# A recurrence's decay exponentials moved ahead of the next tile's gates, with TensorE's order changed to match, and one copy moved in the seventh unit

## The chip, the cores and the metric

The kernel runs on one core of a Trainium2 chip. The metric is the device time of one execution in microseconds (us), as the median of several. The core has five engines that run their own instruction lists in order and meet at semaphores: TensorE (PE in the profile; its weight loads are PEld), VectorE (DVE), ScalarE (ACT), GpSimd (POOL) and SyncE (SP), which here only issues DMAs.

## The reference, cut to what matters

One inference step of a one-layer backbone over 512 latent and 128 context tokens of width 1024. What the change touches is the token mixer:

```python
proj = h @ w_in                               # seven groups of 512 columns
xr, gr, q_raw, ff, fb, iv, og = split(proj)
xc = depthwise_conv(xr, conv_w, conv_b, row_len)
# RG-LRU, forward and backward over the tokens
r = sigmoid(blockdiag(xc, w_a) + b_a); i = sigmoid(blockdiag(xc, w_x) + b_x)
log_a = -8 * r * softplus(-lam);  a = exp(log_a)
u = sqrt(-expm1(2 * log_a)) * (i * xc)
h[t] = a[t] * h[t-1] + u[t]
y_lru = rmsnorm(h_f + h_b) * gelu(gr)
# HGRN2, 4 heads x 2 directions: a chunked gated linear attention
```

Behind it come the output projection, a router and a mixture of 16 experts, which is the longer half of the time.

## The kernel before, in words

Tokens are laid out as 640 columns (512 latent, 128 context); feature channels lie on the 128 partitions. Every engine's list is written out by hand, so the order in the text is the order of the run, and a wait holds up all that is behind it on its engine.

The **first recurrence** (RG-LRU) has four channel tiles j = 0 to 3 and two directions d. For one tile TensorE makes `gates(j, d)`: 16 small products into two PSUM areas. Only (0, 1) has areas of its own, all the others share one pair, so `gates(j, d)` waits until ScalarE has taken the gates before it (`gate_in`). ScalarE's `lru_gates(j)` takes four sigmoids out of PSUM and makes two tanh; `lru_exp(j)` makes the decay `a`, two exponentials; `lru_root(j)` two square roots; `lru_square(j)` the square of the tile's sum for the norm. VectorE's `lru_in(j)` multiplies the input gate by xc, squares the decay (L1645) and forms z (L1648), then `lru_scan(j)` runs the scans (L1655 to L1664) and signals `lru_done`, for which `lru_gates(j + 2)` waits, since tiles j and j + 2 share buffers. VectorE's order is `lru_in(0)`, a swap of halves, `lru_in(1)`, a swap, `lru_scan(0)`, `lru_scan(1)`, and the same for tiles 2 and 3 without the swaps.

TensorE fills the time between gates with the **input projections** of the second recurrence: `HEAD0` = Q, OG, FF, FB, V of head 0, and `EARLY`, the FF of head 1. `project_sample` is 16 matmul instructions of 512 columns (8 steps of k, two instructions each; `range(0, 4)` is half of them), `project_prompt` is 16 of 128 columns and signals `full`. Two PSUM areas alternate; `wait_pa` waits for ScalarE's `projected(item)`, which empties them. `lru_sum` sums the squares over the partitions (it waits for VectorE's `lsq_done`) and feeds the norm's logarithm. On ScalarE `projected(EARLY)` stands just ahead of that logarithm, and it waits for EARLY's `full`:

```python
            act.wait_ge(conv_done, LT + 2)
            projected(EARLY)

            act.wait_ge(ln_ps, 1)
            A(a2[0], p45[:, 0:T], ACT.Ln, bias=eps[:, 0:1], scale=1.0 / (LT * P)).then_inc(ln_log, 1)
```

The **second recurrence** (HGRN2) has eight units u (head u // 2, direction u % 2). In each, ScalarE makes ten exponentials (the last groups are the three `LEVELS`, 64, 32, 16, and W[5]); it copies the turned values out of PSUM (`v_tok`, `vt_done`) and the turned keys (`k_tok`, `kt_done`). TensorE turns the values (`turn_v`, L707), does projections, turns the keys (`turn_k`, L714, into the PSUM area that the values were in, so it waits for `vt_done`), and then `updates`, `scores` and `outputs`. In units 0, 1, 3 and 5 an `ada_copy` on ScalarE feeds an `ada_turn` on TensorE (L621), which stands between the keys and `updates`.

Of the kernel before, what the change touches and what calls it, by code (L numbers as in the profile page):

```python
# [14 lines left out]
KT = D // P  # L15
# [71 lines left out]
def program(nc, x_prompt, x_sample, state_lru, state_hgrn, c, c_ctx, w_ada, b_ada, norm_mix, w_in,  # L87
# [7 lines left out]
    with ctx:  # L95
# [465 lines left out]
        def _(pe):  # L561
# [14 lines left out]
            def project_sample(item, ks=range(KT)):  # L576
                g, j = item
                n, s = USE[item], wait_load(("in", g))
                if ks[0] == 0:
                    wait_pa(n)  # L580
                for k in ks:
                    r = mm(pa[n % 2][:, 0:TS], ring[:, s, k, j * P:(j + 1) * P], hT[:, k, 0:TS], k == 0, k == KT - 1)
                if g == IN_GR and ks[-1] == KT - 1:
                    r.then_inc(full, 1)

            def project_prompt(item):
                g, j = item
                if g == IN_GR:
                    return
                n, s = USE[item], SLOT_OF[("in", g)][0]  # L590
                for k in range(KT):
                    r = mm(pa[n % 2][:, TS:T], ring[:, s, k, j * P:(j + 1) * P], hT[:, k, TS:T], k == 0, k == KT - 1)
                r.then_inc(full, 1)
                if j == HEADS - 1:
                    pe.wait_ge(full, n + 1)
                    pe.sem_inc(freed[s], 1)

            def project(item):
                project_sample(item)
                project_prompt(item)  # L600
# [59 lines left out]
            def gates(j, d):  # L660

                n = 4 * j + 2 * d
                pe.wait_ge(conv_done, (2, 4, 7, 8)[j])
                if n == 0:
                    pe.wait_ge(s_wbd, 16 * 9)
                    pe.wait_ge(xr_in, LT)
                elif n == 2:
                    pe.wait_ge(xr_in, LT)
                else:
                    pe.wait_ge(gate_in, n if n > 4 else 2)  # L670
                for a, b in ((0, TS), (TS, T)):
                    for hf in range(2):
                        for g in range(2):
                            at, out = 64 * (hf ^ g), 64 * hf
                            r = mm(gate_at(j, d, g)[out:out + 64, a:b], wbd[at:at + 64, g, d, j, out:out + 64],
                                   (xc[j], x_swap[j % 2])[g][at:at + 64, a:b])
                r.then_inc(gate_ps, 2)

            def lru_sum():

                pe.wait_ge(lsq_done, LT + 1)
                pe.wait_ge(gate_in, 4 * LT)
                mm(p45[:, 0:TS], ones[:, :], sq[0][:, 0:TS])
                mm(p45[:, TS:T], ones[:, :], sq[0][:, TS:T]).then_inc(ln_ps, 1)
                nc.tensor.transpose(p67[0:8, 0:P], lru_last[:, :, :].rearrange("p d j -> p (d j)"), ident[:, :]).then_inc(lst_ps, 1)
# [174 lines left out]
            gates(0, 0)  # L860
            gates(0, 1)
            gates(1, 0)
            project_sample(HEAD0[0], range(0, 4))
            gates(1, 1)
            project_sample(HEAD0[0], range(4, KT))
            project_prompt(HEAD0[0])
            project(HEAD0[1])
            gates(2, 0)
            project_sample(HEAD0[2])
            gates(2, 1)  # L870
            project_prompt(HEAD0[2])
            gates(3, 0)
            project_sample(HEAD0[3], range(0, 4))
            gates(3, 1)
            project_sample(HEAD0[3], range(4, KT))
            project_prompt(HEAD0[3])
            project(HEAD0[4])
            project(EARLY)
            lru_sum()

            for u in range(UNITS):
                fill = FILL[u]
# [302 lines left out]
        def _(act):  # L1185
# [78 lines left out]
            def lru_gates(j):  # L1264
                b = j % 2
                if j >= 2:
                    act.wait_ge(lru_done, j - 1)
                for d in range(2):
                    for g in range(2):
                        n = 4 * j + 2 * d + g  # L1270
                        act.wait_ge(gate_ps, n + 1)
                        A((rg, ig)[g][b][d], gate_at(j, d, g)[:, 0:T], ACT.Sigmoid,
                          bias=col(("lru_ba", "lru_bx")[g], 4 * d + j)).then_inc(gate_in, 1)
                if j == 0:
                    act.wait_ge(sp_done, 1)
                for d in range(2):
                    act.wait_ge(gate_in, 4 * j + 2 * d + 1)
                    A(th[b][d], rg[b][d], ACT.Tanh, scale=sp[:, 3, 4 * d + j:4 * d + j + 1]).then_inc(gates_done, 1)

            def lru_exp(j):  # L1280
                b = j % 2
                act.wait_ge(gates_done, 2 * j + 2)
                for d in range(2):
                    A(rg[b][d], rg[b][d], ACT.Exp, scale=sp[:, 4, 4 * d + j:4 * d + j + 1]).then_inc(a_done, 1)
# [11 lines left out]
            def projected(item):  # L1296
# [8 lines left out]
                else:  # L1305
                    m = {IN_Q: 2, IN_FF: 0, IN_FB: 1, IN_V: 3}[g]
                    A(raw[h % 2][m], src, ACT.Silu if g == IN_Q else ACT.Copy).then_inc(e, 1)

            lru_gates(0)
            lru_gates(1)  # L1310
            lru_exp(0)
            lru_exp(1)
            projected(HEAD0[0])
            lru_root(0)
            lru_root(1)
            projected(HEAD0[1])
            lru_gates(2)
            lru_gates(3)
            lru_exp(2)
            lru_exp(3)  # L1320
            projected(HEAD0[2])
            lru_square(0)
            lru_square(1)
            lru_root(2)
# [25 lines left out]
            for u in range(UNITS):  # L1350
                h, d = u // 2, u % 2
                rw, fill = raw[h % 2], FILL[u]
                normed = h - 1 if d == 0 and h >= 1 else None
                if u == 0:
                    act.wait_ge(lru_y, 1)
                else:
                    act.wait_ge(o_ps, u)
                if d == 0:
                    for g in (IN_Q, IN_FF, IN_FB, IN_V):
                        n = USE[(g, h)]  # L1360
                        act.wait_ge(empty[n % 2], n // 2 + 1)
                f = rw[d]
                for o, i_ in seq(f, d):
                    r = A(W[6][:, o], i_, ACT.Sigmoid)
                chain(r)
                for o, i_ in seq(f, d):
                    r = A(kk[:, o], i_, ACT.Sigmoid, scale=-1.0)
                chain(r)
                A(lf, W[6], ACT.Ln, bias=lb[:, 4 * d + h:4 * d + h + 1], scale=oml[:, 4 * d + h:4 * d + h + 1]).then_inc(lfk, 1)
                if d == 1:  # L1370
                    for o, i_ in seq(rw[2], d):
                        r = A(rw[1][:, o], i_, ACT.Copy)
                    for o, i_ in seq(rw[3], d):
                        r = A(rw[0][:, o], i_, ACT.Copy)
                    r.then_inc(qrev, 1)
                if normed is not None:
                    head_square(normed)
                    head_log(normed)
                if d == 1 and u < UNITS - 1:
                    projected(fill[0])  # L1380

                act.wait_ge(cum_done, u + 1)
                A(decay[:, :], cum[:, P - 1::P], ACT.Exp)
                act.wait_ge(sub_done, 5 * u + 1)
                A(W[6], W[6], ACT.Exp, scale=-1.0).then_inc(exp_done, 1)
                act.wait_ge(sub_done, 5 * u + 2)
                chain(A(W[4], W[3], ACT.Exp, scale=-1.0))
                A(W[3], W[3], ACT.Exp).then_inc(exp_done, 1)
                for lv, hs in enumerate(LEVELS):
                    act.wait_ge(sub_done, 5 * u + 3 + lv)  # L1390
                    v = W[lv].rearrange("p (g x) -> p g x", x=2 * hs)
                    A(v[:, :, 0:hs], v[:, :, 0:hs], ACT.Exp, scale=-1.0)
                    A(v[:, :, hs:2 * hs], v[:, :, hs:2 * hs], ACT.Exp).then_inc(exp_done, 1)
                A(W[5], cum, ACT.Exp).then_inc(exp_done, 1)
                if normed is not None:
                    head_rstd(normed)
                act.wait_ge(vt_ps, u + 1)
                A(v_tok, p67[:, 0:T], ACT.Copy).then_inc(vt_done, 1)
                if d == 0 or u == UNITS - 1:
                    projected(fill[0])  # L1400
                for item in fill[1:-1]:
                    projected(item)
                act.wait_ge(kt_ps, u + 1)
                A(k_tok, p67[:, 0:512], ACT.Copy).then_inc(kt_done, 1)
                if u in ADA_UNIT:
                    ada_copy(ADA_UNIT[u])
                projected(fill[-1])
# [666 lines left out]
```

## Time and profile before

| | |
|---|---|
| time, median of 3 runs | 1004.91 us (1004.6 to 1005.25) |
| the profiled execution's own time | 1005.39 us, of which the span of the trace is 1003.7 us |
| PE busy | 963.6 us (96%) |
| DVE busy | 362.8 us (36%) |
| ACT busy | 291.8 us (29%), 63 table loads |
| mean granted TensorE clock | 0.992 |

Times in the trace are from the span's start. The first recurrence lies between about 67 us and 138 us, unit 0 of the second between 138 us and 166 us, unit 6 (the seventh) between 321 us and 346 us, and the experts from about 480 us to the end.

### The profile page before, as it was taken

How to read it: one execution, taken by the hardware profiler on the slowest of the kernel's cores; microseconds unless marked ns; L12 is line 12 of the kernel's file. 1: busy time of each engine (PE TensorE's matmuls, PEld its weight loads, DVE VectorE, ACT ScalarE, POOL GpSimd, SP SyncE). 2: the span in 40 equal slices, each digit the busy share in tenths (PEclk: the TensorE clock that was granted, in tenths of full speed). 3: DMA queues.
4: the chain of work that ended last, by engine and by line, in shares of the span. 5: the costliest groups of instructions: out<-in, count | busy, mean ns of one | idle time of the engine just before them, and what ended most of it. 6: DMA issues, size and time to landing. Idle time of an engine off the chain costs nothing.

```text
span 1003.7 us, 18297 instructions
## 1 busy us (share of the span) xinstructions
PE 963.6 (96%) x7982; PEld 429.9 (43%) x7982; DVE 362.8 (36%) x825; ACT 291.8 (29%) x485; POOL 101.8 (10%) x112
## 2 busy tenths in 40 slices
PE   5999899999999899997999999999999999999996
PEld 3555556666666554462232332322323223232232
DVE  4477666463653663663021020210212102112115
ACT  5137756573653754323010010100101001010012
POOL 3200010000000011212001102011010110200100
PEclk9999999999999999999899999999999999999999
DMA  9990013504028441136799999999999999999982
GB/s 332 331 384 7 1 38 142 174 6 169 6 90 316 198 150 73 74 126 238 308 428 403 415 419 411 419 395 415 422 393 418 396 411 416 399 418 401 411 346 105
DMA packets 49396, 276.07 MB, mean 275 GB/s; under 512 B 4001, under 2 KB 12353, under 8 KB 37057
## 3 DMA queue, kind: packets, MB, share of 16 engines
q1 hardware_dynamic: 42000, 253.24, 62.7%
q0 software_dynamic: 5824, 16.81, 5.7%
q10 hardware_dynamic: 1520, 5.28, 1.4%
q8 instruction: 39, 0.64, 0.3%
q14 instruction: 13, 0.10, 0.0%
HBM read 262.30 MB, written 13.01 MB: 274 GB/s over the span
## 4 chain that ended last, share of the span: by engine, by line
PE 83%; DVE 7%; ACT 3%; DMA 3%; issue 2%; POOL 1%; SPq 0%; POOLq 0%; DVEq 0%
PE pa L563 53%; PE p L563 26%; DMA ring<-in_w_ada_dram 1%; ACT reg_c L1195 1%; DMA h_rows<-reg_d 1%; PE pa L1085 1%; ACT L1195 1%; PE p L1023 1%; ACT reg_b L1195 1%; DVE reg_c L1613 1%; DVE reg_c L1658 1%; POOL reg_d L505 0%; ACT reg_d L1195 0%; DMA reg_c<-h_rows,row_s 0%; PE pa L1028 0%
## 5 line engine op out<-in xcount | busy, mean ns | idle before, releaser
L563 PE MATMUL pa<-ring,reg_b 128*32 128x512 f32 (+1 forms) x3232 | 412.8, 595 | 1.3 <-ACT reg_b L1195 1.2
L563 PEld LDWEIGHTS pa<-ring,reg_b 128*32 128x32 f32 (+1 forms) x3232 | 128.6, 114 | 256.5 <-issue 256.0
L563 PE MATMUL pa<-reg_a,ring 128*128 128x512 f32 (+1 forms) x768 | 227.1, 449 | 5.9 <-DVE reg_a L1550 3.3
L563 PE MATMUL p<-ring,reg_b 128*16 128x512 f32 x1536 | 172.7, 594 | 0.0
L563 PEld LDWEIGHTS pa<-reg_a,ring 128*128 128x128 f32 x768 | 118.1, 191 | 98.4 <-issue 98.3
L1195 ACT ACTIVATE reg_b<-pa 128x512 f32<-128x512 f32 (+1 forms) x36 | 21.0, 608 | 426.9 <-PE pa L563 262.6
L563 PEld LDWEIGHTS p<-ring,reg_b 128*16 128x16 f32 x1536 | 44.9, 97 | 121.0 <-issue 120.3
L1952 DVE TENSOR_TENSOR reg_b<-reg_b,p 128x512 f32<-128x512 f32 x8 | 5.5, 687 | 234.4 <-PE p L563 234.4
L1195 ACT ACT_TABLE_LOAD x63 | 80.8, 1283 | 4.1 <-issue 2.8
L1976 DVE SCALAR_TENSOR_TENSOR reg_c<-pa,slot_s,reg_c 128x512 f32<-128x512 f32 x14 | 10.5, 751 | 101.5 <-PE pa L563 101.5
L1195 ACT ACTIVATE reg_c<-reg_c 128x320 f32<-128x320 f32 (+1 forms) x86 | 43.3, 574 | 10.1 <-DVE reg_c L1664 9.2
L541 POOL DMA_INDIRECT sum_rows<-reg_c,row_s x7 | 10.3, 1476 | 262.5 <-DVE reg_c L1976 262.5
L1692 DVE SCALAR_TENSOR_TENSOR reg_c<-reg_c,oml 128x320 f32<-128x320 f32 (+1 forms) x40 | 27.1, 681 | 20.5 <-ACT reg_c L1195 20.5
L1696 DVE TENSOR_TENSOR reg_c<-reg_c 128x640 f32<-128x640 f32 x40 | 30.1, 820 | 0.3
L1983 DVE SCALAR_TENSOR_TENSOR reg_c<-p,slot_q,reg_c 16x512 f32<-16x512 f32 x28 | 20.9, 746 | 20.0 <-PE p L563 19.7
L1960 DVE TENSOR_TENSOR reg_b<-reg_b,pa 128x512 f32<-128x512 f32 x16 | 11.0, 688 | 44.1 <-PE pa L563 44.1
L563 PE MATMUL p<-ring,cs 128*2 128x128 f32 x768 | 24.4, 282 | 2.6 <-DMA ring<-in_w_ada_dram 2.4
L1195 ACT ACTIVATE reg_d<-pa 128x640 f32<-128x640 f32 (+2 forms) x24 | 15.1, 639 | 34.6 <-PE pa L563 34.4
L1692 DVE SCALAR_TENSOR_TENSOR reg_c<-reg_d,reg_c 128x320 f32<-128x320 f32 (+1 forms) x40 | 24.1, 619 | 0.0
L563 PEld LDWEIGHTS p<-ring,cs 128*2 128x2 f32 x768 | 19.5, 87 | 10.7 <-issue 6.4
L1718 DVE TENSOR_TENSOR_SCAN reg_c<-ones,reg_c 128x128 f32<-128x128 f32 x40 | 13.5, 404 | 25.1 <-ACT reg_c L1195 25.1
L563 PE MATMUL p<-reg_c 128*16 128x16 f32 (+3 forms) x640 | 21.6, 202 | 0.0
(304 smaller groups left out, 750.4 us busy)
## 6 DMA issues: line engine op xcount, KB each, us to landing
ring<-in_w_gate_dram SPq DMA_DIRECT2D x32, 2048.0 KB, 13.7
ring<-in_w_up_dram SPq DMA_DIRECT2D x32, 2048.0 KB, 14.1
ring<-in_w_down_dram SPq DMA_DIRECT2D x32, 2048.0 KB, 17.6
ring<-in_w_ada_dram SPq DMA_DIRECT2D x8, 2048.0 KB, 8.2
ring<-in_w_in_dram SPq DMA_DIRECT2D x6, 2048.0 KB, 20.9
ring<-in_w_ada_dram SPq DMA_DIRECT2D x8, 1024.0 KB, 11.5
ring<-in_w_out_dram SPq DMA_DIRECT2D x2, 2048.0 KB, 19.1
sum_rows<-reg_a ACTq DMA_DIRECT2D x5, 512.0 KB, 2.7
```

Source lines behind the costliest of these rows:

```text
L541: pool.indirect_dma_start(sum_rows, bass.IndirectOffsetOnAxis(row_s[0:CS, i:i + 1], 0), out_s[0:CS, :], None, compute_op=ALU.add).then_inc ...
L563: return nc.tensor.matmul(out, lhsT, rhs, start=start, stop=stop, **kw)
L1023: r = nc.tensor.transpose(p67[:, k * P:(k + 1) * P], xg_s[:, k * P:(k + 1) * P], ident[:, :])
L1085: r = nc.tensor.transpose(dst[:, f * P:(f + 1) * P], src[:, f * P:(f + 1) * P], ident[:, :])
L1195: return nc.scalar.activation(out, in_, f, **kw)
L1613: V.scalar_tensor_tensor(dst_s, a_s, wt, dst_s, ALU.mult, ALU.add)
L1692: return V.scalar_tensor_tensor(dst, src, s, dst, ALU.mult, ALU.mult)
L1696: V.tensor_tensor(dst.rearrange("p (g x) -> p g x", x=x), c3, c3[:, :, at:at + 1].to_broadcast([P, T // x, x]), ALU.subtract).then_inc(sub ...
L1718: r = V.tensor_tensor_scan(cum[:, n * P:(n + 1) * P], ones[:, :], lf[:, n * P:(n + 1) * P], 0.0, ALU.mult, ALU.add)
L1960: V.tensor_tensor(in_fours(hv), in_fours(hv), fours(pa[1][:, cols_]), ALU.mult).then_inc(hid_done, 1)
L1976: V.scalar_tensor_tensor(out_s[:, cols_], pa[1][:, cols_], slot_s[:, 1, bass.ds(i, 1)], g2r[0][:, cols_], ALU.mult, ALU.mult).then_inc(out ...
L1983: r = V.scalar_tensor_tensor(out_p[32 * e:32 * e + CP, cols_], p45[rs, 512:1024], slot_q[rs, bass.ds(i, 1)], g2r[1][rs, cols_], ALU.mult, ...
```

## The change

On ScalarE, each tile's two decay exponentials now stand before the next tile's gates, in both pairs of tiles; `projected(HEAD0[2])` stands between tile 2's exponentials and tile 3's gates. On TensorE, the halves between which gates are put are others: Q and FB are projected whole ahead of `gates(1, 1)` and `gates(3, 1)`, FF is split around `gates(2, 1)`, and EARLY's `project_prompt` stands behind `lru_sum`. In unit 6 the copy of the values stands ahead of the last level's exponentials; in the other units it stays where it was.

```diff
             gates(1, 0)
-            project_sample(HEAD0[0], range(0, 4))
+            project_sample(HEAD0[0])
             gates(1, 1)
-            project_sample(HEAD0[0], range(4, KT))
             project_prompt(HEAD0[0])
             project(HEAD0[1])
             gates(2, 0)
-            project_sample(HEAD0[2])
+            project_sample(HEAD0[2], range(0, 4))
             gates(2, 1)
+            project_sample(HEAD0[2], range(4, KT))
             project_prompt(HEAD0[2])
             gates(3, 0)
-            project_sample(HEAD0[3], range(0, 4))
+            project_sample(HEAD0[3])
             gates(3, 1)
-            project_sample(HEAD0[3], range(4, KT))
             project_prompt(HEAD0[3])
             project(HEAD0[4])
-            project(EARLY)
+            project_sample(EARLY)
             lru_sum()
+            project_prompt(EARLY)
...
             lru_gates(0)
+            lru_exp(0)
             lru_gates(1)
-            lru_exp(0)
             lru_exp(1)
             projected(HEAD0[0])
             lru_root(0)
             lru_root(1)
             projected(HEAD0[1])
             lru_gates(2)
+            lru_exp(2)
+            projected(HEAD0[2])
             lru_gates(3)
-            lru_exp(2)
             lru_exp(3)
-            projected(HEAD0[2])
             lru_square(0)
...
+                def values():
+                    act.wait_ge(vt_ps, u + 1)
+                    A(v_tok, p67[:, 0:T], ACT.Copy).then_inc(vt_done, 1)
+
                 for lv, hs in enumerate(LEVELS):
+                    if u == 6 and lv == len(LEVELS) - 1:
+
+                        values()
                     act.wait_ge(sub_done, 5 * u + 3 + lv)
...
-                act.wait_ge(vt_ps, u + 1)
-                A(v_tok, p67[:, 0:T], ACT.Copy).then_inc(vt_done, 1)
+                if u != 6:
+                    values()
```

## Rows read from the trace of the kernel before

**Rows 1.** Timeline of VectorE, first recurrence: start, length, engine, line, operation, [idle before].
```profile
81.65 0.83 DVE L1645 TENSOR_TENSOR reg_d<-reg_c 128x640 f32<-128x640 f32 x1 [8.86 <-ACT reg_c L1195]
...
91.55 0.83 DVE L1655 TENSOR_TENSOR reg_c<-reg_c 128x640 f32<-128x640 f32 x1
...
121.54 0.82 DVE L1655 TENSOR_TENSOR reg_c<-reg_c 128x640 f32<-128x640 f32 x1
```

**Rows 2.** Timeline of ScalarE, tiles 0 and 1.
```profile
71.42 1.56 ACT L1195 ACTIVATE reg_c<-reg_c,sp 128x640 f32<-128x640 f32 x2
...
79.50 1.28 ACT L1195 ACT_TABLE_LOAD   x1
80.79 1.55 ACT L1195 ACTIVATE reg_c<-reg_c,sp 128x640 f32<-128x640 f32 x2
```

**Rows 3.** Timeline of ScalarE, tiles 2 and 3.
```profile
97.52 1.48 ACT L1195 ACTIVATE reg_c<-p,pv 128x640 f32<-128x640 f32 x2 [2.94 <-DVE reg_c L1664]
...
108.61 1.48 ACT L1195 ACTIVATE reg_b<-p,pv 128x640 f32<-128x640 f32 x2 [3.33 <-PE p L563]
...
112.83 1.55 ACT L1195 ACTIVATE reg_c<-reg_c,sp 128x640 f32<-128x640 f32 x2
...
116.31 0.72 ACT L1195 ACTIVATE reg_b<-reg_c 128x640 f32<-128x640 f32 x1
...
118.97 1.36 ACT L1195 ACTIVATE reg_c<-reg_c 128x640 f32<-128x640 f32 x2
```

**Rows 4.** Timeline of TensorE, first recurrence.
```profile
71.56 3.70 PE L563 MATMUL pa<-reg_a,ring 128*128 128x512 f32 x8
...
91.74 7.13 PE L563 MATMUL pa<-reg_a,ring 128*128 128x512 f32 x16
...
100.38 2.05 PE L563 MATMUL pa<-reg_a,ring 128*128 128x128 f32 x16
...
107.23 0.64 PE L563 MATMUL p<-reg_c,reg_e 64*64 64x512 f32 x1
...
136.45 1.35 PE L563 MATMUL p<-reg_b,ones 128*128 128x512 f32 x4 [2.36 <-DVE reg_b L1679]
```

**Rows 5.** Timeline of ScalarE, the norm's logarithm and unit 0.
```profile
137.84 0.79 ACT L1195 ACTIVATE reg_d<-p,eps 128x640 f32<-128x640 f32 x1 [1.65 <-PE p L563]
...
158.51 0.60 ACT L1195 ACTIVATE reg_c<-p 128x512 f32<-128x512 f32 x1 [0.44 <-PE p L714]
159.01 0.38 ACT L1195 ACTIVATE ada_sb<-p 128x256 f32<-128x256 f32 x1
```

**Rows 6.** Timeline of TensorE, unit 0: the turn that waits for the last copy.
```profile
160.10 0.38 PE L621 MATMUL p<-ident,ada_sb 128*128 128x128 f32 x2
```

**Rows 7.** Timeline of TensorE, unit 6.
```profile
337.25 0.63 PE L714 MATMUL p<-ident,reg_c 128*128 128x128 f32 x4 [2.29 <-ACT reg_e L1195]
337.72 2.74 PE L563 MATMUL pa<-reg_a,ring 128*128 128x512 f32 x6
```

**Rows 8.** Timeline of ScalarE, unit 6.
```profile
331.00 4.90 ACT L1195 ACTIVATE reg_c<-reg_c 128x640 f32<-128x640 f32 x10
...
336.43 0.68 ACT L1195 ACTIVATE reg_e<-p 128x640 f32<-128x640 f32 x1
...
338.92 0.59 ACT L1195 ACTIVATE reg_c<-p 128x512 f32<-128x512 f32 x1
```

**Rows 9.** TensorE by stretches: stretch, its length, busy (instructions), granted clock, DMA share, GB/s.
```profile
134.00:136.00 2.00, 0.09 (x1) 1.00 0.00 0
```

**Rows 10.** All engines by stretches: length, PE, PEld, DVE, ACT, POOL busy, granted clock, DMA.
```profile
16.00:20.00 4.00, 3.62 (x69) 2.53 (x69) 0.00 (x0) 0.28 (x1) 0.00 (x0) 0.62 1.09 357
...
476.00:480.00 4.00, 2.72 (x20) 1.34 (x23) 1.62 (x8) 0.00 (x0) 2.31 (x3) 0.55 0.94 290
480.00:484.00 4.00, 4.00 (x28) 0.90 (x24) 0.23 (x2) 0.60 (x1) 0.00 (x0) 0.59 0.43 167
```

**Rows 11.** Waits between 370 us and 482 us, TensorE's longest.
```profile
PE p L1028 <- DMA reg_c<-h_rows,row_p: 4.1, 1, 4.1
```

## The prediction

> **What bounds the kernel now.** I read the chain of waits first: outside the first recurrence it is nearly all TensorE, so there a saving counts only if it makes TensorE start earlier, and any delay of TensorE is kept. Inside the first recurrence, from 67 us to 137 us, the chain goes between the engines, and I read the timelines of VectorE, ScalarE and TensorE side by side. What the reader is to see: VectorE stands idle 8.86 us before tile 0's decay is squared at 81.65 us [rows 1], because ScalarE makes tile 0's exponentials only after tile 1's gates, at 80.79 us [rows 2]. The wait comes again in the second pair, whose exponentials start at 112.83 us [rows 3]. From the first scan of tile 2 at 121.54 us [rows 1] VectorE works without a gap up to the sum for which TensorE waits at 136.45 us, having idled 2.36 us [rows 4]. So the end of this stage is set by the start of that scan, and 136.45 - 121.54 = 14.9 us behind it are fixed. Call S what happens to the scan's start; the sum of the change hangs on it.
>
> **Tiles 0 and 1.** Tile 0's tanh end at 71.42 + 1.56 = 73.0 us. A table load takes 1.28 us and a pair of exponentials 1.55 us, with nothing between them [rows 2]. So the exponentials now run from 74.3 to 75.8 us, a second new load ends at 77.1 us, and a pair of sigmoids (1.48 us [rows 3]) at 78.6 us. TensorE meanwhile projects Q whole: half takes 3.7 us, the whole 7.1 us until gates can follow [rows 4], so from 71.6 us to 78.7 us; both engines are ready at once there. `gates(1, 1)` costs 1.3 us (107.23 us to ScalarE's start at 108.61 us [rows 3, 4]), so ScalarE starts the sigmoids at 80.1 us. From those sigmoids to the exponentials behind them it is 112.83 - 108.61 = 4.22 us, load included [rows 3]: tile 1's exponentials start at 84.3 us and end at 85.8 us. Two loads and Q's SiLU (0.7 us) later, at 89.1 us, comes the first root, 0.7 us long, so the scan of tile 0 can start at 89.8 us. VectorE has four operations of 0.8 us after the first exponential at 85.1 us and a swap of 1 us, and is ready at 89.3 us. The scan was at 91.55 us [rows 1]: 1.7 us gained.
>
> **Tiles 2 and 3.** Tile 2's sigmoids wait for tile 0's sum, so they come 1.7 us sooner than 97.52 us [rows 3], at 95.8 us, and end at 97.3 us. `gates(2, 1)`, now behind only half of FF, runs at once, to 98.7 us. ScalarE: sigmoids at 98.8 us, exponentials 4.22 us later at 103.0 us, done 104.55 us; FF's copy (0.7 us), a load, and the sigmoids of `gates(3, 0)` end at 108.0 us. TensorE from 98.7 us: half of FF 3.6, its prompt part 2.0 [rows 4], `gates(3, 0)` 1.25, which is 105.5 us; then FB whole, 7.1, which is 112.6 us; only then `gates(3, 1)`, done at 113.9 us. This is the step that costs: ScalarE has freed the area at 108.0 us, and TensorE comes 4.6 us later, where the kernel before had it at 107.23 us [rows 4]. Sigmoids at 113.95 us, exponentials 4.22 us later from 118.2 to 119.7 us, two squares and a table load, 118.97 - 116.31 = 2.66 us [rows 3], and 0.7 us for the first root: 123.05 us. VectorE could start at 119.0 + 3.2 = 122.2 us, so ScalarE sets it. Against 121.54 us S is **+1.5 us**. Bounds: the whole 4.6 us cut away gives S = -3.0 (exponentials at 113.6 us, root done at 118.5 us); half a microsecond of slips on the way gives +2.0. I take +1.5.
>
> **The sum and EARLY's prompt part.** `lru_sum` moves to 137.95 us. Before, EARLY's prompt part was done ahead of it, and TensorE idled; now its 1.8 us (2.0 less the overlap [rows 4]) stand behind it. TensorE alone is then 1.5 + 1.8 = 3.3 us late. What is queued behind it matters more: on ScalarE `projected(EARLY)` stands ahead of the norm's logarithm and waits for that prompt part. `lru_sum` 1.35 [rows 4] ends at 139.3 us, the prompt part at 141.1 us, the copy 0.7 us later, and the table load that was hidden in the 1.65 us of waiting [rows 5] now follows it: logarithm at 143.1 us instead of 137.84 us [rows 5], **5.25 us late**. ScalarE and VectorE go from there to unit 0's keys without slack. In unit 0 ScalarE waited 0.44 us at 158.51 us, so it could copy from 158.07 us; the two copies take 0.88 us, 158.95 us [rows 5], and TensorE used the second at 160.10 us [rows 6]. Slack 1.15 us: 5.25 - 1.15 = **4.1 us** is what TensorE loses by the end of unit 0, and it holds TensorE's own 3.3 us. From there on TensorE has no idle in which to win it back.
>
> **Unit 6.** TensorE waits 2.29 us for the values before the keys are turned at 337.25 us [rows 7]. The ten exponentials run from 331.00 to 335.9 us, one more follows, and the copy starts at 336.43 us [rows 8]. By my estimate of 0.63 us for a whole one and 0.38 us for a half (4 and 6 of them make 4.8), the copy stands 0.63 + 0.63 + 0.76 = 2.0 us earlier, and the keys turn at 335.1 us. But the copy of the keys stays behind all the exponentials and a GELU, and ends at 338.92 + 0.59 = 339.5 us [rows 8], where `updates` started at 337.72 + 2.74 = 340.46 us [rows 7]. So of 2.1 us only **0.8 us** is gained. The last level comes 0.6 us later; VectorE has not yet come to it then, so this costs nothing.
>
> **The granted clock.** TensorE will finish EARLY's latent part at about 132.7 us (roots to 125.1 us, FB's copy to 125.8 us, 6.9 us of matmul) and then idle until 137.95 us, 5.2 us. The clock stayed at 1.00, its 2.4 GHz level, through the 2.36 us of idle around 134 us [rows 4, 9]. After the 4.1 us wait for gathered rows [rows 11] it was lower, with a mean of 0.55 and then 0.59 over 8 us [rows 10], that is mostly at the 1.2 GHz level. 5.2 us is past the wait after which it fell. Bounds: nothing, and (0.45 + 0.41) x 4 = 3.4 us. At 16 to 20 us, where matmul work followed at once as it will here, 1.5 us of clock went, of which 0.2 us in idle [rows 10]: I take **+1.3 us**. It delays sum and prompt part and so both paths alike.
>
> The Trainium skill, TensorE: Matmul & The Clock Gate, section on the clock gate, says that the throttled state is the default and that idling brings it back; by that rule the 1.3 us stand, and rows 10 agree with it.
>
> **The sum.** +4.1 - 0.8 + 1.3 = +4.6 us. The profiled execution, 1005.39 us, becomes 1010.0 us; the median of the runs lies 0.5 us below it, 1004.91 us, and becomes **1009.5 us** (+0.46%).
>
> **The four further table loads.** They are 5.1 us of ScalarE by the rows, and fall where ScalarE is level with TensorE (first pair) or ahead of it (second), so they are in the sum only through the 78.6 us and 108.0 us above.
>
> The Trainium skill, ScalarE: Activation LUTs, section Rules for kernel authors, says to do all of one table set before switching, and puts a switch at about 2.7 us, the load and a drain. Here the next activation starts 0.01 us after the load's 1.28 us [rows 2], so the trace doesn't bear the drain out.
>
> **The rivals.** (a) *The clock does not fall*: +3.3 us, 1008.2 us. For it: the one wait after which it fell is not much shorter than this, and had other work around it. (b) *Not slower*: TensorE reaches `gates(3, 1)` as soon as the area is free, at about 108.1 us. Then S is -3.0 us, the logarithm 5.25 - 4.5 = 0.75 us late, unit 0 0.75 - 1.15 = -0.4 us, with unit 6 -1.2 us: 1003.7 us. It decides once `gates(3, 1)` starts before about 109 us. Against it: the 7.1 us of FB are in rows 4, and the lists are in order. Even this does not reach 0.2%. (c) *The late tile 3 is absorbed in part*, S = 0: the logarithm is still 3.75 us late through EARLY, unit 0 +2.6 us, with unit 6 +1.8 us: 1006.7 us. (d) *A switch of tables costs ScalarE 1.4 us more than its row*. Two of them lie before `gates(1, 1)`'s area is free, 2.7 us later than TensorE, and all behind moves: +7.3 us, 1012.2 us. The row against it is the one above.
>
> The Trainium skill, ScalarE: Activation LUTs, section What ACT_TABLE_LOAD costs, is where (d)'s price stands: about 1.4 us of drain behind each load.
>
> **How the numbers follow.** Forecast 0.42, (a) 0.28, (b) 0.10, (c) 0.15, (d) 0.05. About 0.2% (2 us) is what a measurement here can tell from no change. (b) and half of (c) lie inside it or below: faster 0.05, which is (b) with some further gain, same 0.15, slower 0.80. The range of 8 in 10 takes in (a), the upper half of (c) and the clock's upper bound less what seldom comes together: 1006.2 to 1011.3 us. The forecast's own range, with (a), is 1007.6 to 1011.3 us.
>
> **What the changed profile would show.** Tile 0's squares on VectorE at about 75 us with 2 to 3 us of idle ahead, and the first scan of tile 0 near 89.8 us. `gates(3, 1)` near 112.6 us, with ScalarE idle some 6 us ahead of its last sigmoids. The first scan of tile 2 near 123 us; `lru_sum` near 138 us after some 5 us of idle; the logarithm some 5 us later than before, and a granted clock below 1 around 138 us. In unit 0 the turn of L621 waits for ScalarE. In unit 6 the wait of 2.29 us is gone and `updates` waits for the keys' copy. The prediction is wrong if TensorE comes to `gates(3, 1)` early, if the logarithm does not wait for EARLY, or if TensorE has room later in which the delay is lost.

## The result, and the profile after

The changed kernel took 1012.34 us (median of 7 runs, 1008.09 to 1014.57) beside 1005.25 us (7 runs, 1004.18 to 1007.12) of the kernel before: ratio 1.0058, 95% interval 1.0044 to 1.0071, which is 5.8 us (4.4 to 7.1) slower. The prediction was 1009.5 us, within 1006.2 to 1011.3 us. The median lies 1.0 us above that range; the ratio puts the change at 4.4 to 7.1 us slower, and the forecast of 4.6 us is near the lower end of that. The profiled execution took 1008.09 us with a span of 1006.4 us. It is the fastest of the seven, and its span is only 2.7 us over that of the kernel before; the rows show what was in it, and what by luck was not.

VectorE in the first recurrence, timeline of the changed kernel (columns as in [rows 1]; L1653 here is L1645 before, L1663 is L1655):

```profile
74.08 0.83 DVE L1653 TENSOR_TENSOR reg_d<-reg_c 128x640 f32<-128x640 f32 x1 [2.38 <-ACT reg_c L1195]
...
88.94 0.82 DVE L1663 TENSOR_TENSOR reg_c<-reg_c 128x640 f32<-128x640 f32 x1 [0.60 <-ACT reg_c L1195]
...
114.38 0.83 DVE L1650 TENSOR_TENSOR reg_b<-reg_b,reg_c 128x640 f32<-128x640 f32 x1 [6.07 <-ACT reg_b L1195]
117.95 0.82 DVE L1653 TENSOR_TENSOR reg_d<-reg_b 128x640 f32<-128x640 f32 x1 [2.75 <-ACT reg_b L1195]
122.04 0.83 DVE L1663 TENSOR_TENSOR reg_c<-reg_c 128x640 f32<-128x640 f32 x1 [0.93 <-ACT reg_c L1195]
```

In the kernel before, the second pair's wait was as long as the first's:

```profile
113.69 0.83 DVE L1645 TENSOR_TENSOR reg_d<-reg_c 128x640 f32<-128x640 f32 x1 [8.88 <-ACT reg_c L1195]
```

The two waits of 8.9 us are gone. In the first pair that gains 1.5 us: the first scan's product comes 22.7 us after the first gates (88.94 - 66.26) where it came after 24.2 us. In the second pair the wait is only cut into parts, of which the long ones, 6.07 and 2.75 us, stand ahead of tile 3 instead of tile 2: the product comes after 55.8 us instead of 54.2 us, later than before.

TensorE, timeline of the changed kernel, beside [rows 4]:

```profile
66.26 0.61 PE L563 MATMUL p<-reg_c,reg_e 64*64 64x512 f32 x1 [0.95 <-DVE reg_c L1622]
...
96.54 0.61 PE L563 MATMUL p<-reg_c,reg_e 64*64 64x512 f32 x1 [2.02 <-ACT reg_c L1195]
97.78 5.49 PE L563 MATMUL pa<-reg_a,ring 128*128 128x512 f32 x24
...
104.43 7.13 PE L563 MATMUL pa<-reg_a,ring 128*128 128x512 f32 x16
111.49 0.64 PE L563 MATMUL p<-reg_c,reg_e 64*64 64x512 f32 x1
...
136.95 2.50 PE L563 MATMUL p<-reg_b,ones 128*128 128x512 f32 x4 [5.29 <-DVE reg_b L1687]
139.24 0.42 PE L685 MATMUL p<-ident,lru_last 128*8 128x128 f32 x1
```

`gates(2, 1)` now waits 2.02 us for its area. FB's 16 instructions run whole from 104.43 us, so `gates(3, 1)` starts only at 111.49 us, and ScalarE waits 5.48 us for it:

```profile
112.87 1.48 ACT L1195 ACTIVATE reg_b<-p,pv 128x640 f32<-128x640 f32 x2 [5.48 <-PE p L563]
```

`lru_sum` comes after 5.29 us of idle and takes 2.50 us instead of 1.35. The granted clock tells why (stretch, length, busy, clock, as in [rows 9]):

```profile
130.00:132.00 2.00, 1.66 (x4) 1.00 0.00 0
...
134.00:136.00 2.00, 0.00 (x0) 0.50 0.00 0
136.00:138.00 2.00, 1.05 (x2) 0.50 0.00 0
138.00:140.00 2.00, 2.00 (x8) 0.50 0.00 0
140.00:142.00 2.00, 2.00 (x16) 0.82 0.01 2
```

TensorE was busy at the 2.4 GHz level until it went idle near 131.7 us. By 134 us it was granted the 1.2 GHz level, and came back to full only after 140 us, under `lru_sum` and EARLY's prompt part. The Trainium skill, TensorE: Matmul & The Clock Gate, section What's actually happening, gives the throttled state as the default to which the clock returns after idling; the trace agrees, with 0.50 after 5.29 us of idle.

ScalarE, the norm's logarithm and unit 0's last copies, beside [rows 5]:

```profile
142.11 0.70 ACT L1195 ACTIVATE reg_d<-pa 128x640 f32<-128x640 f32 x1 [7.51 <-PE pa L563]
142.83 1.28 ACT L1195 ACT_TABLE_LOAD   x1
144.12 0.80 ACT L1195 ACTIVATE reg_d<-p,eps 128x640 f32<-128x640 f32 x1
...
164.25 0.59 ACT L1195 ACTIVATE reg_c<-p 128x512 f32<-128x512 f32 x1
164.73 0.39 ACT L1195 ACTIVATE ada_sb<-p 128x256 f32<-128x256 f32 x1
```

EARLY's copy, then the load, then the logarithm, in a row with no gap: the copy waited 7.51 us for the prompt part that now stands behind `lru_sum`. In unit 0 TensorE waits for the last copy, where before ScalarE was ahead [rows 6]:

```profile
165.18 0.44 PE L621 MATMUL p<-ident,ada_sb 128*128 128x128 f32 x2 [0.28 <-ACT ada_sb L1195]
```

Unit 6 on TensorE, beside [rows 7]:

```profile
340.41 0.63 PE L714 MATMUL p<-ident,reg_c 128*128 128x128 f32 x4 [0.33 <-ACT reg_e L1195]
340.88 2.74 PE L563 MATMUL pa<-reg_a,ring 128*128 128x512 f32 x6
344.69 0.49 PE L563 MATMUL p<-reg_e,reg_c 128*128 128x128 f32 x2 [1.08 <-ACT reg_c L1195]
```

The 2.29 us of waiting for the values have become 0.33 us, and 1.08 us for the keys have come in their place.

The first gates start at a different moment in each execution (65.8 to 67.8 us after the start, in these profiles), so the stages are compared by distances from the first gates. From there to the turn of L621 it is 92.8 us before and 98.9 us after, +6.2 us (differences here are formed before rounding). From the turn to the first router logits it is 230.3 and 229.7 us, -0.6 us. Together that is +5.6 us. The span shows 2.7, mainly because the first gates came 1.1 us earlier in this execution, and because in the wait for gathered rows ahead of the experts (4.1 us before [rows 11]) it had this:

```profile
PE p L1028 <- DMA reg_c<-h_rows,row_p: 3.2, 1, 3.2
```

That wait is 0.9 us shorter, and behind it 1.7 us of clock was lost where the profile before lost 3.4 (summed as one less the granted clock, over stretches of 2 us). I put both down to the execution and not to the change: the kernel of e2 below, which has the same first recurrence, waits 3.75 us there and loses 3.4 us in its profile.

### The profile page after: what moved, and what is told of

It reads as the page before. It is cut to its first block, busy times and chain, and to the rows that moved or that the text cites. A ratio compares the mean times of both kernels' runs of the same rounds, so it can differ in the third digit from the quotient of the medians.

```text
span 1006.4 us, 18301 instructions
## 1 busy us (share of the span) xinstructions
PE 964.5 (96%) x7982; PEld 431.5 (43%) x7982; DVE 363.1 (36%) x825; ACT 296.6 (29%) x489; POOL 101.1 (10%) x112
## 4 chain that ended last, share of the span: by engine, by line
PE 81%; DVE 6%; ACT 6%; DMA 3%; issue 2%; POOL 1%; SPq 0%; POOLq 0%; ACTq 0%; DVEq 0%
PE pa L563 52%; PE p L563 25%; ACT reg_c L1195 2%; ACT L1195 1%; DMA ring<-in_w_ada_dram 1%; ACT reg_b L1195 1%; DMA h_rows<-reg_d 1%; ACT reg_d L1195 1%; PE pa L1085 1%; PE p L1023 1%; DVE reg_c L1621 1%; DVE reg_c L1666 1%; POOL reg_d L505 0%; DMA reg_c<-h_rows,row_s 0%; PE pa L1028 0%
## 5 line engine op out<-in xcount | busy, mean ns | idle before, releaser
L1700 DVE SCALAR_TENSOR_TENSOR reg_c<-reg_d,reg_c 128x320 f32<-128x320 f32 (+1 forms) x40 | 24.2, 622 | 0.0
L563 PE MATMUL p<-reg_c,reg_e 128*128 128x128 f32 (+2 forms) x120 | 18.4, 359 | 3.7 <-ACT reg_c L1195 2.6
```

The lines of the kernel that those rows point to most:

```text
L563: return nc.tensor.matmul(out, lhsT, rhs, start=start, stop=stop, **kw)
L1700: return V.scalar_tensor_tensor(dst, src, s, dst, ALU.mult, ALU.mult)
```

## The experiments

There are twelve kernels. They ran in three groups, each on a chip of its own beside runs of the kernel before (medians there 1005.65, 1005.45 and 1005.83 us). What is compared is the ratio to those runs, in brackets with its 95% interval, and its difference from one is given in us. Kernels of different groups, and the change itself, are compared by these ratios.

**e1, unit 6 alone.** The kernel before with

```diff
+                def values():
+                    act.wait_ge(vt_ps, u + 1)
+                    A(v_tok, p67[:, 0:T], ACT.Copy).then_inc(vt_done, 1)
+
                 for lv, hs in enumerate(LEVELS):
+                    if u == 6 and lv == len(LEVELS) - 1:
+                        values()
...
-                act.wait_ge(vt_ps, u + 1)
-                A(v_tok, p67[:, 0:T], ACT.Copy).then_inc(vt_done, 1)
+                if u != 6:
+                    values()
```

> The kernel before with only the values' copy of unit 6 moved. Theory: the wait of 2.3 us ahead of the keys' turn goes, updates come 0.6 to 0.8 us sooner, and the rare fall of the clock in that wait goes with it: faster than before by 0.6 to 0.9 us. Rival, that the late last level takes it back: no difference.

Measured 1004.74 us, ratio 0.9991 (0.9983 to 1.0): 0.9 us faster, at the edge of what the runs can tell. Its profile shows the same 0.32 us and 1.07 us of waiting as above, and 0.6 us less from the turn of L621 to the logits.

**e2, the recurrence alone.** The change with the values' copy of unit 6 where it was.

```diff
-                    if u == 6 and lv == len(LEVELS) - 1:
+                    if False:
...
-                if u != 6:
-                    values()
+                values()
```

> The change without its edit in unit 6. Theory (late gates of tile 3, EARLY's prompt part ahead of the logarithm, and the clock): unit 6 is worth 0.6 to 0.8 us, so this is slower than the kernel before by 6.4 us where the whole change was by 5.8. Rival, that moving the values' copy does harm by making the last level late: less than 5.8 us slower.

Measured 1012.68 us, ratio 1.0079 (1.0058 to 1.01): 7.9 us slower. The rival is not borne out, though the interval begins at its 5.8 us; e1 speaks against it too. In its profile the wait of 2.29 us in unit 6 brought the clock down:

```profile
340.00:342.00 2.00, 0.00 (x0) 0.93 0.98 418
342.00:344.00 2.00, 2.00 (x6) 0.50 0.12 49
344.00:346.00 2.00, 2.00 (x4) 0.71 0.01 4
```

From the turn of L621 to the logits it is 231.9 us here and 229.7 us in the changed kernel, so in an execution with this fall the edit in unit 6 saves 2.2 us and not 0.6.

**e3, EARLY's prompt part first.**

```diff
-            project_sample(EARLY)
+            project(EARLY)
             lru_sum()
-            project_prompt(EARLY)
```

> The change, with EARLY's prompt part ahead of lru_sum as before. Theory: the first scan of tile 2 stays 1.5 us late, but the logarithm is late only by that, not by 5.25 us; TensorE +1.5 us, unit 6 -0.6 us, and idle ahead of lru_sum 3.5 us instead of 5.3, after which the clock may or may not fall: slower than before by 0.9 us with a full clock and up to 2.5 us without. Rival, that the four added table loads are the cost: slower by 5 to 6 us as with the whole change.

Measured 1008.71 us, ratio 1.0037 (1.0023 to 1.0052): 3.7 us slower. That is 1.2 us over the upper end of the theory, which the interval still takes in, and below the rival's 5 to 6 us, which only the interval's end touches (e5 decides that). The logarithm follows `lru_sum` again at once. But its profile shows a thing the theory lacked, the clock around the new wait ahead of `gates(2, 1)`:

```profile
97.66 0.91 PE L563 MATMUL p<-reg_c,reg_e 64*64 64x512 f32 x1 [2.02 <-ACT reg_c L1194]
```

```profile
94.00:96.00 2.00, 1.64 (x4) 1.00 0.00 0
96.00:98.00 2.00, 0.34 (x4) 0.96 0.00 0
98.00:100.00 2.00, 2.00 (x17) 0.50 0.03 8
100.00:102.00 2.00, 2.00 (x4) 0.68 0.00 0
```

After two microseconds of idle the gates and the start of FF's second half run at the 1.2 GHz level (0.50). The first scan of tile 2 came 1.6 us later for it than in the changed kernel's own profile, where the same wait left the clock up.

**e4, FB split.**

```diff
-            project_sample(HEAD0[3])
+            project_sample(HEAD0[3], range(0, 4))
             gates(3, 1)
+            project_sample(HEAD0[3], range(4, KT))
             project_prompt(HEAD0[3])
```

> The change, with FB split in halves around gates(3, 1) as before. Theory: gates(3, 1) starts 3.4 us earlier, the first scan of tile 2 is 1.9 us ahead of the kernel before instead of 1.5 us late; the logarithm is still 3.75 us behind that, +1.9 us, unit 0 +0.7 us, unit 6 -0.6 us: +0.1 us, and up to 1.5 us more where the clock falls in the 3 us of idle. Rival (table loads are the cost): slower by 5 to 6 us.

Measured 1008.58 us, ratio 1.0029 (1.0018 to 1.004): 2.9 us slower. Half of the loss goes with FB's place, but the theory's upper end was 1.6 us and the interval begins at 1.8: it is a miss. In the profile the clock fell twice, after the 2.02 us ahead of `gates(2, 1)`, which the theory did not count, and after 3.22 us ahead of `lru_sum`, each time by 1.7 us.

**e5, both repairs** (the diffs of e3 and e4 together).

> The change with both repairs: FB split around gates(3, 1), and EARLY's prompt part ahead of lru_sum. Theory: first scan of tile 2 and lru_sum 1.9 to 2.1 us ahead of the kernel before, unit 6 another 0.6 us: faster by 2.6 us with a full clock, by 1.0 us where the clock falls in the 2 us wait ahead of gates(2, 1), which this keeps. Rival (the table loads, or the exponentials' place itself): slower.

Measured 1001.92 us, ratio 0.9972 (0.996 to 0.9984): 2.8 us faster than before. All four added table loads and the early exponentials are in it (67 loads against 63), so the rival is out. Its profile has the fall at `gates(2, 1)` and is 0.8 us faster from the first gates to the logits, about the theory's 1.0 us; the runs, 1.6 to 4.0 us faster, show more, and why stays open.

**e6, a filler ahead of EARLY.**

```diff
+            s = wait_load(("in", IN_FF))
+            wait_pa(USE[EARLY])
+            for k in range(6):
+                mm(pa[1][:, 0:TS], ring[:, s, k, P:2 * P], hT[:, k, 0:TS])
             project_sample(EARLY)
             lru_sum()
```

> The change, with 12 matmul instructions whose result is overwritten put ahead of EARLY's latent part, so that TensorE is busy nearly up to lru_sum; nothing else moves. It does 5.15 us of matmul more than the change. Theory with the clock: lru_sum starts at the same time but at a full clock, so it is slower than before by 3.5 us and not by 5.8, and its runs lie closer together. Rival without the clock: slower by 5.8 us as the change, or more, as TensorE does more work.

Measured 1009.25 us, ratio 1.0038 (1.0023 to 1.0053): 3.8 us slower, with 12 more matmul instructions, where the change was 5.8 us slower; the two intervals overlap, so by these runs alone the difference is not certain. The runs span 1.4 us (6 runs) where the change's span 6.5 us. `lru_sum` ran at full clock. The filler did not touch the wait ahead of `gates(2, 1)`, and the clock fell there in its profile.

**e7, the logarithm first on ScalarE.**

```diff
-            act.wait_ge(conv_done, LT + 2)
-            projected(EARLY)
-
             act.wait_ge(ln_ps, 1)
...
             A(a2[0], a2[0], ACT.Exp, scale=-0.5).then_inc(ln_rstd, 1)
+            act.wait_ge(conv_done, LT + 2)
+            projected(EARLY)
```

> The change, with EARLY's copy on ScalarE put behind the norm's logarithm and exponential; TensorE's list is untouched. Theory: the logarithm is then late by lru_sum alone (1.5 us and the clock), and what is left is TensorE's own delay of 3.3 us less 0.6 us of unit 6, and the clock's 1 to 3 us: slower than before by 4 to 5 us, about 1 us less than the whole change. Rival, that only the ScalarE order matters and TensorE's delay is hidden: slower by 1 to 2.5 us.

Measured 1011.12 us, ratio 1.0048 (1.003 to 1.0066): 4.8 us slower, which can't be told from the change's 5.8 us. In its profile the logarithm follows `lru_sum` at once and the trace shows no wait of TensorE between `lru_sum` and the turn of L621, yet that turn comes after 100.6 us: 1.7 us later than in the changed kernel, with one fall of the clock (1.7 us) more. So TensorE's own delay stands close behind ScalarE's.

**e8, TensorE's order alone.** The change, with ScalarE's order of the kernel before and unit 6 as before.

```diff
             lru_gates(0)
-            lru_exp(0)
             lru_gates(1)
+            lru_exp(0)
...
             lru_gates(2)
-            lru_exp(2)
-            projected(HEAD0[2])
             lru_gates(3)
+            lru_exp(2)
             lru_exp(3)
+            projected(HEAD0[2])
...
-                    if u == 6 and lv == len(LEVELS) - 1:
+                    if False:
...
```

> The change's order on TensorE with ScalarE's order of the kernel before, unit 6 as before. Theory, by the sum of the rows: gates(1, 1) 3.5 us late and gates(3, 1) 10 us late with nothing on ScalarE that gains by it; lru_sum 10 us late, the logarithm 14 us, so 12 to 14 us slower. Rival (TensorE's order is neutral, the table loads cost): no slower than 1 us.

Measured 1021.73 us, ratio 1.0155 (1.014 to 1.017): 15.6 us slower, 1.6 us over the theory's upper end, whose 14 us is also where the interval begins. I had counted no fall of the clock; in its profile the first recurrence holds waits such as these, and the clock fell in both and again after 2.77 us ahead of `lru_sum`:

```profile
101.26 1.08 PE L563 MATMUL p<-reg_c,reg_e 64*64 64x512 f32 x1 [7.14 <-ACT reg_c L1195]
128.50 11.99 PE L563 MATMUL pa<-reg_a,ring 128*128 128x512 f32 x36 [6.02 <-ACT reg_d L1195]
```

**e9, ScalarE's order alone.** The change's ScalarE list with TensorE's list of the kernel before, unit 6 as before.

```diff
-            project_sample(HEAD0[0])
+            project_sample(HEAD0[0], range(0, 4))
             gates(1, 1)
+            project_sample(HEAD0[0], range(4, KT))
...
-            project_sample(HEAD0[2], range(0, 4))
+            project_sample(HEAD0[2])
             gates(2, 1)
-            project_sample(HEAD0[2], range(4, KT))
...
-            project_sample(HEAD0[3])
+            project_sample(HEAD0[3], range(0, 4))
             gates(3, 1)
+            project_sample(HEAD0[3], range(4, KT))
...
-            project_sample(EARLY)
+            project(EARLY)
             lru_sum()
-            project_prompt(EARLY)
...
-                    if u == 6 and lv == len(LEVELS) - 1:
+                    if False:
...
```

> The change's order on ScalarE with TensorE's order of the kernel before, unit 6 as before. Theory: FF whole ahead of gates(2, 1) and Q split leave gates(3, 1) waiting 2.7 us for its area, first scan of tile 2 and lru_sum 2.1 us late, EARLY in place: 2 us slower with a full clock, up to 3.5 us where it falls in the wait of 2.7 us. Rival (the table loads are the whole cost): 5 to 6 us slower.

Measured 1009.76 us, ratio 1.0032 (1.0019 to 1.0045): 3.2 us slower. Its profile, of the slowest of the five runs, has waits of 3.52 us ahead of `gates(1, 1)`, which the theory had not counted, and 2.51 us ahead of `gates(3, 1)`; the clock fell in both, and again in the wait of 2.29 us in unit 6.

**e10, both repairs, and FF split six to two.** As e5, and

```diff
-            project_sample(HEAD0[2], range(0, 4))
+            project_sample(HEAD0[2], range(0, 6))
             gates(2, 1)
-            project_sample(HEAD0[2], range(4, KT))
+            project_sample(HEAD0[2], range(6, KT))
```

> As e5, with FF split six and two steps around gates(2, 1) instead of four and four. Theory: TensorE is busy until the area is free, so the wait ahead of gates(2, 1) is 0.2 us and not 2.0 us, the clock stays up there, and gates(3, 1) comes another 0.9 us sooner: faster than before by 3.6 us, with runs closer together than e5's. Rival, that the wait of 2 us has nothing to do with the clock: 0.9 us faster than e5 at the same spread.

Measured 1001.74 us (1001.18 to 1002.41 in 5 runs), ratio 0.9965 (0.9952 to 0.9978): 3.5 us faster than the kernel before, 9.3 us faster than the change by the ratios. e5's six runs span 2.8 us, these five 1.2 us; the medians of the two are not apart, so what the split of six to two adds to e5 is shown by the profile alone. TensorE:

```profile
91.06 5.42 PE L563 MATMUL pa<-reg_a,ring 128*128 128x512 f32 x12
96.77 0.61 PE L563 MATMUL p<-reg_c,reg_e 64*64 64x512 f32 x1 [0.29 <-ACT reg_c L1195]
...
102.94 3.70 PE L563 MATMUL pa<-reg_a,ring 128*128 128x512 f32 x8
107.42 0.61 PE L563 MATMUL p<-reg_c,reg_e 64*64 64x512 f32 x1 [0.78 <-ACT reg_b L1195]
...
132.87 1.35 PE L563 MATMUL p<-reg_b,ones 128*128 128x512 f32 x4 [1.42 <-DVE reg_b L1687]
```

No wait of this stretch is over 1.5 us, and the clock is 1.00 throughout; `lru_sum` takes its 1.35 us again.

**e11, two fillers.** e6 and, in the second bank of FF's area ahead of its prompt part,

```diff
             project_sample(HEAD0[2], range(0, 4))
+            s = wait_load(("in", IN_FF))
+            for k in range(2):
+                mm(pa[0][:, 512:1024], ring[:, s, k, 0:P], hT[:, k, 0:TS])
             gates(2, 1)
```

> As e6, with four more overwritten matmul instructions in the 2 us wait ahead of gates(2, 1). Theory: with the clock kept up there too, the first scan of tile 2 is 1.5 us late in every run, where in e6's profile it was 3.2 us late: 0.8 us faster than e6 on the mean, so slower than before by 2.9 us. Rival, that the wait does not matter: as e6, 3.6 us.

Measured 1009.27 us, ratio 1.0031 (1.0021 to 1.0042): 3.1 us slower. By the runs it can't be told from e6, but its interval, 2.1 to 4.2 us, lies wholly below the change's 4.4 to 7.1. By the profile it is the change with the clock taken out:

```profile
97.58 0.61 PE L563 MATMUL p<-reg_c,reg_e 64*64 64x512 f32 x1 [0.30 <-ACT reg_c L1202]
```

```profile
164.41 0.44 PE L621 MATMUL p<-ident,ada_sb 128*128 128x128 f32 x2 [0.28 <-ACT ada_sb L1202]
```

Its first gates were at 67.32 us, so the turn of L621 comes after 97.1 us.

**e12, EARLY alone.** The kernel before with

```diff
-            project(EARLY)
+            project_sample(EARLY)
             lru_sum()
+            project_prompt(EARLY)
```

> The kernel before with one edit: EARLY's prompt part behind lru_sum. Theory: lru_sum stays in place, the logarithm is 3.75 us late, of which unit 0 takes up 1.15: 2.6 us slower with a full clock; TensorE now idles 4.2 us ahead of lru_sum, and where the clock falls there it is 1 to 2 us more, so 2.6 to 4.5 us. Rival, that EARLY costs only its own 1.8 us of TensorE: 1.8 us slower.

Measured 1011.95 us, ratio 1.0058 (1.0046 to 1.0071): one moved call costs as much as the whole change. The theory's upper end was 4.5 us, and the interval begins at 4.6. The profile bears the theory out, 4.4 us to the turn of L621, with this:

```profile
117.01 17.23 PE L563 MATMUL pa<-reg_a,ring 128*128 128x512 f32 x48 [2.59 <-ACT reg_d L1196]
136.92 2.40 PE L563 MATMUL p<-reg_b,ones 128*128 128x512 f32 x4 [2.67 <-DVE reg_b L1680]
```

The clock fell in each of these two waits (0.65, then 0.50, at 116 to 120 us; 0.77, 0.50 and 0.88 at 136 to 142 us). The first fall cost about 1.5 us of what would have been idle ahead of `lru_sum`, which is why the second wait is 2.67 us and not the theory's 4.2. What the runs show beyond the profile's 4.4 us, 1.4 us with an interval from 0.2 to 2.7, stays open.

Where the profiles stand, in us from an execution's first gates; the scan is the operation behind the product shown above, the last column but one is where the first router logits stand, and lost clock is the sum of one less the granted clock from 64 us to 150 us after the start:

```
                        first scan   lru_sum's  logarithm  turn of  router  clock
                        of tile 2    transpose             L621     logits  lost
before                    55.1        70.3       70.5       92.8    323.1   0
e1 unit 6 alone           55.1        70.3       70.5       92.8    322.4   0
after                     56.6        73.0       77.9       98.9    328.6   3.4
e2 recurrence alone       56.6        73.0       77.9       99.0    330.9   3.4
e11 two fillers           56.6        71.9       76.0       97.1    326.8   0
e6 filler                 58.3        73.5       77.7       98.8    328.5   1.7
e3 EARLY first            58.3        74.6       74.9       98.9    328.6   5.1
e4 FB split               54.9        71.2       75.9       96.9    326.7   3.4
e7 logarithm first        58.3        74.6       74.9      100.6    330.2   5.1
e5 both repairs           54.9        70.1       70.3       92.6    322.2   1.7
e10 both, FF six          52.3        67.5       67.7       90.0    319.7   0
e9 ScalarE's order        61.2        76.5       76.7       98.9    330.9   5.1
e12 EARLY alone           55.1        71.3       76.1       97.2    327.5   3.4
e8 TensorE's order        68.4        84.7       89.4      110.5    340.8   9.3
```

The distances say where the time goes, and the runs how much it is. The profile of the kernel before lost no clock in this stretch, and its runs span 2.4 to 4.4 us, so the distances of a profile with many falls can lie above what the runs show (e7: 7.2 us by the logits, 4.8 us by the runs).

## Why the prediction was right, and where a size was off

**Tiles 0 and 1.** Forecast 1.7 us gained at tile 0's scan; 1.5 measured. By itself it is worth nothing, as the second pair decides.

**S.** Forecast +1.5 us for the first scan of tile 2; the profile after and e11, both with a full clock there, show +1.6. `gates(3, 1)` was forecast 45.3 us after the first gates (112.6 - 67.34) and came after 45.2. That FB ahead of `gates(3, 1)` is the cause is shown by e4 against e3: with FB split the first scan stands at 54.9 us, with FB whole at 58.3, both with one fall of the clock ahead; that is the 3.4 us of half a projection.

**EARLY.** Forecast 5.25 us for the logarithm with a full clock; e11 shows 5.5 (76.0 - 70.5). Forecast +4.1 us at unit 0's turn; e11 shows +4.3 (97.1 - 92.8). e12 shows that this place alone suffices for a loss of this size. e7 shows that the two paths through it lie close together, as the sum had them (3.3 us of TensorE within the 4.1): taking one away leaves the other. e3 and e4, each with one of the two steps left, are slower than the kernel before, and e5 and e10, without both, are faster: both steps have to go.

**Unit 6.** Forecast -0.8 us; -0.6 us in the profiles after and of e1. The working took 340.46 us, the end of the rows ahead, for the start of `updates`; the trace of the kernel before has it at 340.30 us.

**The clock.** Here the size was off. Forecast +1.3 us, at `lru_sum`. That fall measured 98.9 - 97.1 = 1.8 us, after against e11. The step that failed is the sentence that `gates(2, 1)` "runs at once": it runs after 2.0 us of idle, which was in the sum as time and not as a danger to the clock, for a wait of 2.36 us had left it at 1.00 [rows 9]. In the seven profiles with that wait (after, e2 to e7), whose lists are the same up to there, the clock fell in it in five, all but after and e2, and a fall costs 1.6 us at the first scan (58.3 against 56.6, before rounding). Five in seven of 1.6 is 1.2 us on the mean; that is an estimate from few profiles. The full-clock terms measured 4.3 - 0.6 = 3.7 us, and with 1.8 and 1.2 that is 6.7 us, inside the measured 4.4 to 7.1. The runs agree: e11, which removes both falls and adds 16 matmul instructions, is 3.1 us slower than the kernel before where the change is 5.8, so the clock is worth 2.7 us there, against 1.8 + 1.2 = 3.0 by the profiles and the forecast's 1.3.

**The rivals.** (a), no fall at `lru_sum`, did not come in any of the three profiles that had the 5.3 us wait (after, e2, e7). (b), gates in time, did not come either; e10 shows what it is worth when it is arranged, with the first scan 2.8 us earlier than before where (b) had 3.0. (c), S absorbed, did not come: S was +1.6 us. (d), each table switch dearer than its row, is out by the rows after: the activation follows the load's 1.28 us at once, at 144.12 us behind the load of 142.83. e5 and e10 have the same loads and are faster than the kernel before. The Trainium skill, ScalarE: Activation LUTs, section Table sets: the hidden batching unit, advises to batch by table set; here two loads more per pair were worth it, once TensorE's list matched (e5, e10).

The order of ScalarE alone loses 3.2 us (e9) and that of TensorE alone 15.6 us (e8), so the two orders do belong together; what cost the time is how TensorE's was matched to it in two places, FB and EARLY.

## What to carry to other kernels

When an engine's work is moved forward, work out anew at which moment each of the other engines comes to the hand-over; a piece of filling work in eight steps can be split anywhere. Here FF split six and two and FB four and four, with EARLY's part back ahead of the sum (e10), was 9.3 us faster than the change with FF four and four, FB whole and EARLY's part behind the sum; nearly all of that is FB's and EARLY's, as e5 shows.

A piece moved behind a sum to fill time can cost more than its own length when another engine has a wait for it ahead of its own next step. Here 1.8 us of work made the logarithm 3.9 us later (5.5 less the 1.6 of the scan). Look through every list for who waits for the moved piece, and what is queued behind that wait.

Price a TensorE wait of the lengths in which the clock was seen to fall, here from 2.0 us up, with the clock behind it, as a chance and not as a yes or no.

## What the runs showed of the hardware that was not expected

A TensorE wait of 2.0 us was followed by the 1.2 GHz level in five of seven profiles and left 2.4 GHz in two. The wait of 2.3 us in unit 6 left the clock up in three profiles (before, e8, e12) and brought it down in two (e2, e9); the wait of 2.6 us ahead of V left it up in before and e1 and brought it down in e12. Over all fourteen profiles, from the first gates to the logits and the gathered rows, the clock fell in 11 of 20 waits of 2.0 to 2.8 us, and in all 22 of 3.18 us and more. So one profile of a clean wait of two to three microseconds says little.

The same list with 12 matmul instructions added (e6) ran 2.0 us faster than without, by the ratios, and with 16 added (e11) 2.7 us faster; only the second is clear of noise. Most falls cost 1.7 us of clock, or 3.4 us, in these profiles, with little between; the one behind the 7.14 us wait of e8 cost 5.1 us.
